# Last output projection with tokens on partitions, normalised and stored block by block

## The reference

```python
            u = rms_norm_2(h, sb_norm_pre[j])
            proj = u @ sb_w_in[j]
            q, g = jnp.split(proj, [SB_QK_WIDTH], axis=-1)
            q = split_heads(q, SB_HEADS).astype(jnp.float32)
            o = stick_breaking_attention(q, k_shared, v_shared)
            o = merge_heads(o).astype(h.dtype) * jax.nn.silu(g)
            y = o @ sb_w_out[j]
            h = h + rms_norm_2(y, sb_norm_post[j])      # returned

def rms_norm_2(x, g):
    xf = x.astype(jnp.float32)
    y = xf * lax.rsqrt(jnp.mean(xf * xf, axis=-1, keepdims=True) + EPS)
    return (y * g.astype(jnp.float32)).astype(x.dtype)
```

## Time and profile before

| | us |
|---|---|
| median of 3 runs | 2039.12 (2038.88 to 2039.78) |
| the profiled execution, in all | 2041.25 |
| its span, first to last instruction | 2039.4 |
| TensorE busy | 1968.8 (97%) |
| VectorE busy | 1189.2 (58%) |
| ScalarE busy | 701.1 (34%) |
| GpSimd busy | 11.3 (1%) |

### The profile page before, as it was taken

One profiled execution on the slowest core, in us unless ns is written; L12 is line 12 of the kernel. 1 busy time (PEld: TensorE's weight loads), 2 busy tenths in 40 slices (PEclk: granted clock), 3 DMA queues, 4 the chain that ended last, 5 costly groups with the idle time before them and its releaser, 6 DMA issues.

```text
span 2039.4 us, 24203 instructions
## 1 busy us (share of the span) xinstructions
PE 1968.8 (97%) x9308; PEld 1660.7 (81%) x9308; DVE 1189.2 (58%) x1424; ACT 701.1 (34%) x750; POOL 11.3 (1%) x19
## 2 busy tenths in 40 slices
PE   6999999999999999999999999999996999999995
PEld 5888888789797788888888888888885788888884
DVE  5433445676655566343355658484959665555557
ACT  4322323234333333223232333232324544444443
POOL 0000000000000000000000000000000000000000
PEclk9999999999999999999999999999998999999998
DMA  4222232311202222222223322221212122222211
GB/s 172 85 103 103 69 100 89 131 47 42 78 1 84 90 104 100 103 85 100 90 85 99 128 83 93 72 103 67 98 62 83 42 83 83 71 74 82 82 62 42
DMA packets 27414, 171.78 MB, mean 84 GB/s; under 512 B 3184, under 2 KB 3200, under 8 KB 10464
## 3 DMA queue, kind: packets, MB, share of 16 engines
q1 hardware_dynamic: 25344, 165.95, 23.3%
q0 software_dynamic: 864, 2.99, 0.4%
q10 hardware_dynamic: 1152, 2.10, 0.3%
HBM read 168.93 MB, written 2.10 MB: 84 GB/s over the span
## 4 chain that ended last, share of the span: by engine, by line
PE 88%; DVE 7%; ACT 3%; issue 1%; DMA 0%; DVEq 0%; ACTq 0%
PE acc L1365 26%; PE acc L1367 26%; PE acc L1366 26%; PE att L1365 2%; PE att L1367 2%; PE att L1366 2%; ACT w_hi L352 1%; DVE w_lo L742 1%; DVE rstd L795 1%; PE att L1713 1%; PE att L1712 1%; ACT tmp L466 1%; DVE neg_max L919 0%; PE acc L1525 0%; DMA h<-in_x 0%
## 5 line engine op out<-in xcount | busy, mean ns | idle before, releaser
L1365 PE MATMUL acc<-x_hi,w_hi 128*128 128x512 f32 x1408 | 555.2, 394 | 17.5 <-DVE w_lo L742 15.4
L1366 PE MATMUL acc<-x_lo,w_hi 128*128 128x512 f32 x1408 | 549.9, 391 | 0.0
L1367 PE MATMUL acc<-x_hi,w_lo 128*128 128x512 f32 x1408 | 549.9, 391 | 0.0
L742 DVE TENSOR_TENSOR w_lo<-raw,w_hi 128x2048 fp32r<-128x2048 f32 (+1 forms) x166 | 378.4, 2280 | 141.3 <-ACT w_hi L352 137.2
L352 ACT ACTIVATE w_hi<-raw 128x2048 fp32r<-128x2048 f32 (+1 forms) x166 | 315.1, 1898 | 107.6 <-PE acc L1367 103.0
L1365 PEld LDWEIGHTS acc<-x_hi,w_hi 128*128 128x128 f32 x1408 | 265.6, 189 | 75.6 <-DVE w_lo L742 15.4
L1366 PEld LDWEIGHTS acc<-x_lo,w_hi 128*128 128x128 f32 x1408 | 265.5, 189 | 57.2 <-issue 2.4
L1367 PEld LDWEIGHTS acc<-x_hi,w_lo 128*128 128x128 f32 x1408 | 265.4, 189 | 55.9
L1366 PE MATMUL acc<-g_lo,w_hi 128*128 128x512 f32 x352 | 136.9, 389 | 0.0
L1365 PE MATMUL acc<-g_hi,w_hi 128*128 128x512 f32 x352 | 136.9, 389 | 0.0
L1367 PE MATMUL acc<-g_hi,w_lo 128*128 128x512 f32 x352 | 136.9, 389 | 0.0
(11 more groups left out here) (279 smaller groups left out, 2916.6 us busy)
## 6 DMA issues: line engine op xcount, KB each, us to landing
raw<-in_ffn_up SPq DMA_DIRECT2D x44, 1024.0 KB, 4.7
raw<-in_ret_head SPq DMA_DIRECT2D x24, 1024.0 KB, 4.7
raw<-in_ffn_down SPq DMA_DIRECT2D x32, 704.0 KB, 4.1
raw<-in_mix_gate SPq DMA_DIRECT2D x8, 1024.0 KB, 4.7
raw<-in_ret_out SPq DMA_DIRECT2D x8, 1024.0 KB, 4.7
raw<-in_sb_v SPq DMA_DIRECT2D x8, 1024.0 KB, 4.8
raw<-in_sb_kq SPq DMA_DIRECT2D x8, 1024.0 KB, 4.7
raw<-in_sb_g SPq DMA_DIRECT2D x8, 1024.0 KB, 4.7
```

The source lines that it names most:

```text
L742: tt(w_lo[:, slot, 0:cols], raw[:, slot, 0:cols], w_hi[:, slot, 0:cols].bitcast(F32), ALU.subtract).then_inc(w_ready, 1)
L1365: mm(dst, still[0], move[0], start=first, stop=False)
L1366: mm(dst, still[0], move[1], start=False, stop=False)
L1367: return mm(dst, still[1], move[0], start=False, stop=last)
```

## The change

The last head's output projection is turned round, so that tokens lie on the partitions. To make the sum over heads possible, the output projection of every head is: the stationary side is now the high or low part of `so` for 128 tokens, and the moving side 512 columns of the weights (`out_passes`). Chunk j of `y_sb` is now block m = j // 2 of 128 tokens and half j % 2 of the width; the count of matmuls and their shape stay. `sb_w_out` is laid out accordingly by the host code.

- The residual h is needed with tokens on partitions too. `turn_h` transposes it on TensorE: for each j four 128x128 tiles into one side bank, 32 tiles in all. ScalarE copies each bank to `h_tok` (`take_turned`). `h_tok` takes the place of kv_hi and kv_lo, which are read no more by then.
- Four banks are turned between the output projection of head 7 and the value products of the last head, two after these, and two in the middle of the last projection.
- The last projection does blocks 0 and 1 (four banks) with the loop over k outside, so that it can start when `so_lo` of the first half is there, and then blocks 2 and 3 one bank after another.
- For each block ScalarE squares 1024 columns with a row sum (`accum_out`), and takes a root over one column. Its table is loaded early, by a root of `eps` in the last head.
- GpSimd multiplies blocks 0 to 2 by the gain rows in place, VectorE block 3. VectorE takes the reciprocal of one column and does y times rstd plus h in one operation per half (`finish`), and SP stores each half.
- In the last head VectorE puts `sp_lo` ahead of the last add, and `so_lo` of the first half ahead of the gate of the second.

The diff, without the declarations:

```diff
             for c in range(DC):
                 sp.wait_ge(h_ready, 3 * DC + c + 1)
-                sp.dma_start(out[:, c, :], h[:, c, :]).then_inc(out_landed, 16)
+                sp.dma_start(out[:, c, :], h_tok[:, c, :]).then_inc(out_landed, 16)
...
+            pool.wait_ge(h_ready, 2 * DC + 1)
+            pool.dma_start(gain_rows[:], dram["gain_rows"]).then_inc(gain_landed, 16)
+            pool.wait_ge(gain_landed, 16)
+            for m in range(TB - 1):
+                pool.wait_ge(act_step, 2 * SB_HEADS + 1 + m + 1)
+                rows = slice(2 * m, 2 * m + 2)
+                nc.gpsimd.tensor_tensor(by_rows(y_sb[:, rows, :]), by_rows(y_sb[:, rows, :]), gain_rows[:], ALU.mult).then_inc(y_gained, 1)
...
+            def take_turned(first, end):
+                for j in range(first, end):
+                    act.wait_ge(h_turned, j + 1)
+                    nc.scalar.activation(h_tok[:, j, :], att[:, b.k % BANKS, :], ACT.Copy).then_inc(h_tok_ready, 1)
+                    b.next()
...
                 sb_weights()
-                if not last:
+                if last:
+                    take_turned(0, TB)
+                    nc.scalar.activation(std_tok[:, 0:1], eps[:], ACT.Sqrt, bias=eps[:]).then_inc(act_step, 1)
+                    step.next()
+                else:
                     sb_kq()
                 sb_gated()
...
-            for c in range(DC):
-                act.wait_ge(acc_free, u.next() + BANKS)
-                square(c, y_sb[:, c, :])
-            std_of()
+            take_turned(TB, TB + SB_VC)
+            for m in range(TB):
+                act.wait_ge(acc_free, u.next(2) + BANKS)
+                at = 2 * TOK * (m % 2)
+                nc.scalar.activation(tmp[:, at:at + 2 * TOK], by_rows(y_sb[:, 2 * m:2 * m + 2, :]), ACT.Square,
+                                     accum_out=sq_tok[:, m:m + 1]).then_inc(act_step, 1)
+                act.wait_ge(act_step, step.next())
+                nc.scalar.activation(std_tok[:, m:m + 1], sq_tok[:, m:m + 1], ACT.Sqrt, bias=eps[:],
+                                     scale=1.0 / D).then_inc(fn_ready, 1)
+                if m == 0:
+                    take_turned(TB + SB_VC, DC)
...
                 if last:
-                    sb_out(DC // 2, DC)
+                    b.next(TB)
+                    sb_out(DC // 2, DC - 1)
                 low(sp_lo[:], e, sp_hi[:])
-                if not last:
+                if last:
+                    sb_out(DC - 1, DC)
+                else:
                     sb_kq()
...
+            def finish(m, y):
+                dve.wait_ge(fn_ready, fn.next())
+                link(nc.vector.reciprocal(rstd_tok[:, m:m + 1], std_tok[:, m:m + 1]))
+                dve.wait_ge(h_tok_ready, 2 * m + 2)
+                for half in range(2):
+                    row = h_tok[:, 2 * m + half, :]
+                    stt(row, y[:, TOK * half:TOK * half + TOK], rstd_tok[:, m:m + 1], row, ALU.mult, ALU.add).then_inc(h_ready, 1)
+
             settle()
-            squared.next(DC)
-            for c in range(DC):
-                sb_out(c, c + 1)
-                if c:
-                    sum_square(c - 1)
-            sum_square(DC - 1)
-            post_norm(y_sb, 8, True)
+            last_gained = tmp[:, 4 * TOK:6 * TOK]
+            for m in range(TB):
+                sb_out(2 * m, 2 * m + 2)
+                if m:
+                    dve.wait_ge(y_gained, m)
+                    finish(m - 1, by_rows(y_sb[:, 2 * m - 2:2 * m, :]))
+            dve.wait_ge(gain_landed, 16)
+            dve.wait_ge(acc_free, u.at(BANKS))
+            link(tt(last_gained, by_rows(y_sb[:, DC - 2:DC, :]), gain_rows[:], ALU.mult))
+            finish(TB - 1, last_gained)
...
+            def out_passes(dst, w, j, k):
+                m, half = divmod(j, 2)
+                return passes(dst, (so_hi[:, k, plain[m]], so_lo[:, k, plain[m]]), w(2 * k + half, TOK),
+                              k == 0, k == SB_VC - 1)
...
+            def turn_h(first, end, taken):
+                for j in range(first, end):
+                    m, half = divmod(j, 2)
+                    if taken:
+                        pe.wait_ge(h_tok_ready, j - SB_VC + 1)
+                    dst = side_bank()
+                    for i in range(TB):
+                        done = nc.tensor.transpose(dst[:, P * i:P * i + P], h[:, TB * half + i, plain[m]], ident[:])
+                    done.then_inc(h_turned, 1)
...
                 if last:
-                    sb_out(w, DC // 2)
+                    sb_out(w, DC // 2, DC)
+                    turn_h(0, TB, False)
...
             sb_body(False, True)
-            pe.wait_ge(op_ready, op.at())
-            sb_out(slab())
-            sq.next(DC)
-            mean_square()
+            turn_h(TB, TB + SB_VC, True)
+            w = slab()
+            dst = [bank() for _ in range(BANKS)]
+            for k in range(SB_VC):
+                pe.wait_ge(op_ready, op.at(k - SB_VC + 1))
+                for j in range(BANKS):
+                    done = out_passes(dst[j], w, j, k)
+                    if k == SB_VC - 1:
+                        done.then_inc(seg_done, 1)
+            turn_h(TB + SB_VC, DC, False)
+            sb_out(w, BANKS, DC)
```

57 lines of the change are left out of this document (41 added, 16 removed).

## The result

The changed kernel took 2024.09 us (median of 4 executions, 2023.74 to 2026.20) against 2039.45 of the kernel before beside it on the same chip (4 executions); the ratio is 0.9926, with a 95% interval of 0.9909 to 0.9944. The forecast was 2027.2 with a range of 2024.0 to 2032.0, so the change gained 3 us more than forecast, and the time lies 0.09 us inside the range's lower end. The sum of the prediction holds in most of its steps, but two of its numbers were wrong, in opposite directions, and 4.4 us came from a place that it had costed at nothing.

What follows compares the result with a forecast made beforehand. TensorE was taken to bound the body, waits and a serial chain the last 41 us. 2.0 us won by the last matmul and 9.9 after it make 11.9, off the median 2039.12: 2027.2, range 2024 to 2032 (0.84).

Steps and rivals of the forecast that it cites:

- TensorE up to the last matmul: Last head: both waits and the slow half go, 24 transposes come in; last matmul 2.0 us earlier (2019.27 to 2017.29).
- both waits: TensorE's idle 2.2 us before the last head's value products and 2.16 us before the last projection; both forecast to go.
- The clock, first rival: Last head's value products: transposes don't hold the clock, 1.55 us comes back, 2029.1; chance 0.34 shared with collision and two-record transposes.
- The projections, "cost nothing": Output projections, all eight heads: so stationary, weights moving costs nothing (392 ns against 390), same 48 matmuls a head.
- my own list: Signs of being wrong: GpSimd products over 3 us, projections' 0.227 pace changing in any head, tail longer than 14 us.
- The tail: After the last matmul: squares, gain products and finishes block by block, 20.1 us down to 10.2, 9.9 won.
- finish(0): Tail, first block: reciprocal of 0.16 and two fused operations of 0.744 on VectorE, 1.67 us with handovers, ending 2015.47.
- The second rival: Tail: GpSimd's product waits until VectorE's fused pair is through, end 2028.8; chance 0.34 shared with clock and two-record transposes.
- third: Tail: GpSimd's first two-input product pays 6 us once, all on the chain, end 2033.5; chance 0.07.
- fourth: Tail: slower than before through VectorE's wait for y_gained; gain gone from 12 us extra on the first product; chance 0.02.
- fifth rival: Tail: stores still bunch at the end or another wait fills it, time near today's; needs 8 us of waiting; chance 0.04.
- all sizes at their good ends: Unknown sizes, such as GpSimd's product and the transposes, all at their low ends: span ends at 2024.0.

## Why the prediction was right where it was, and wrong where not

- **TensorE up to the last matmul.** Forecast 2.0 us won, measured 2.80 (stretch B). The order of the steps was right: no idle, both halves at full clock in 3.88 us (forecast 3.92). Too dear were the transposes: 24 of them in 2.48 us, 0.103 a tile where I took 0.133 (0.71 us in all). By the Trainium skill ("TensorE: Matmul & The Clock Gate", Terms) I had given an estimate of 0.07; the measurement lies between. The trace of before had no row for it.
- **What brought the 2.8.** I put it to a swap of both waits against 24 transposes. The order of sp_lo alone gives as much (25.49 against 25.48): without the rest of the change the wait for so_lo stays (2.17 us there), with it the time is spent on turning h, which the new tail needs. Nothing in the rows ties the two sums together, so that they come out equal is taken as chance.
- **The clock, first rival.** It didn't come true: the granted clock is 1.00 over the transposes and behind them. The Trainium skill ("TensorE: Matmul & The Clock Gate", Part 4) has it that transposes don't count as activity as matmuls do. These runs neither show nor exclude that: TensorE was without matmuls for 1.66 us here, and the clock also held with most of the transposes gone; it fell after waits of 2.17 and 2.18 us, and not after each of them.
- **The projections, "cost nothing".** True for the form that I checked: 512 columns moving with so stationary keeps 227 ns. But the step failed in what it left out. I costed the change's instructions and not its allocation, which moved kv by a distance that isn't a multiple of 256 and won 4.4 us in a form that I hadn't named (120 to 113.5 ns). It is the larger miss, and shown by both directions, one with no instruction changed. By my own list I would be wrong "if the projections' pace of 0.227 changes in any head"; at 512 columns that pace held, but for the 192 matmuls with kv moving (227 before; medians of 226, 229 and 232 after, 64 matmuls each), and the form that moved the time stood on no list.
- **The tail.** Forecast from the last matmul's start to the last VectorE operation 8.1 us, measured 10.07. GpSimd's product was 2.41 (forecast 2.3), the square with its read 1.16 on the chain (forecast 1.25), the reciprocal 0.16, the gain product 1.22, the end 2.5: all close to what I had sized. From the end of the adds of block 2 to the end of finish(2) it was 5.37 us forecast and measured. The one term that failed is finish(0): 1.67 forecast, 3.57 measured from 2008.96 to 2012.53, because its first operation was held 1.9 us.
- **The second rival was right in kind and wrong in direction.** I let GpSimd's product wait for VectorE's pair (+1.3 us); it was the pair that waited for the product (+1.9). I had the second product start 0.5 us behind the pair's release (2014.3 against 2013.8), since ScalarE's two copies and its square of block 1 come first; these were done at 2008.75, before the first product was (2008.95), so the second product follows at once and runs for 0.26 us when the pair begins. That the rival stood beside a forecast that ignored it was a choice for which the trace gave no row. The Trainium skill ("SBUF — State Buffer", Who interferes with whom) says that a VectorE instruction with two SBUF inputs contends with a GpSimd one that reads SBUF, that one with at most one such input does not (outside the 2-port modes), and that the one that starts first holds the other off. The runs agree where GpSimd's came first: pairs 3.34, 4.33 and 2.01 and a product of 2.70 were held, adds of 0.69 were not, nor was the one beside the fill. Where VectorE's came first the runs show less: the third product of the changed kernel began 0.26 us before a pair's end and took 2.46 instead of 2.39.
- **The third, fourth and fifth rival** did not come true: the first product took 2.40, and the results are stored from 2011.9 on.

In sum, for the profiled execution: 11.9 forecast, plus 0.8 on TensorE, less 1.96 in the tail, plus 4.4 from the address of kv, makes 15.1; the spans differ by 15.0. In the part that I had costed, 0.8 and 1.96 partly cancel: with kv on the grid the change gives 2028.41, 1.2 above the forecast, and that the two nearly meet is in part luck. The 4.4 us took the time to the lower end of the range, where I had put kernels with all sizes at their good ends; it got there for another reason.

## What to carry to other kernels

Count an edit's allocations among its parts: if a change moves an operand of TensorE by anything but a multiple of 512 bytes (shifts by such multiples left every pace here alone), compare the start-to-start pace of every form that uses it, also in stages that the change doesn't touch, and try a pad both ways. Before work goes to GpSimd to relieve VectorE, look at what VectorE does meanwhile: operations with both inputs in SBUF stood still here until GpSimd's running product was through, and three products of 2.4 us there cost more here than 1.23 each on VectorE. Where executions differ by more than the effect, time the stretch that the edit touches, not the whole.

## What the runs showed that I had not expected

- The placement of a matmul's operands relative to each other in SBUF changes its pace: 113.5 to 120 ns at 256 columns, 225 to 236 at 512, same instructions. Moving only w by 64 bytes cost 39 us of 2024.
- A VectorE operation that was held ended 0.55 us behind GpSimd's instruction (the rows of 2.70 and 4.33 us). GpSimd pays too, though less: three products in a row took 7.52 us where VectorE waited from the second on, and 7.25 where it waited for the third alone.
- The best order found, all finishes after the last add, is 1.0 us shorter in its own stretch than the changed kernel, and leaving GpSimd out gives the same 1.0; together they weren't tried.
